# Head gates of the block-key mixer: three products of rounded halves in place of one full-precision product

## The reference

```python
xn = rmsnorm(x, mix_norm[i])
proj = xn @ w_in                      # 256 x 1024 times 1024 x 2608
q, kc, vc, ks, vs, kw, vw, gates = jnp.split(proj, cuts, axis=-1)
gates = jax.nn.sigmoid(gates.reshape(bsz, s, g, r, 3) + b_gate.reshape(g, r, 3))
```

## Time and profile before

| | us |
|---|---|
| median of 3 runs (lowest, highest) | 2112.36 (2108.29, 2113.53) |
| the profiled execution, its own time | 2112.04 |
| its span, first to last instruction | 2110.2 |
| PE busy in the span | 2084.3 (99%) |
| DVE busy | 1541.8 (73%) |
| ACT busy | 1289.6 (61%) |
| POOL busy | 61.5 (3%) |

### The profile page before, as it was taken

The page is one execution under the profiler, slowest core; times in us unless marked ns, Lnnn a source line. Parts: engine busy times, 40 slices in busy tenths (PEclk is TensorE's granted clock), DMA queues, the critical chain, the costliest instruction groups (busy, mean ns, idle before and its releaser), DMA issues.

```text
span 2110.2 us, 33620 instructions
## 1 busy us (share of the span) xinstructions
PE 2084.3 (99%) x12545; PEld 1790.8 (85%) x12545; DVE 1541.8 (73%) x2787; ACT 1289.6 (61%) x2170; POOL 61.5 (3%) x51
## 2 busy tenths in 40 slices
PE   8999999999999999999999999999999999999999
PEld 7888988888888877888888897888887888988887
DVE  6777888677766677766877677587677776868676
ACT  6656766556555367655665677565565555666555
POOL 0001000000000400000000001000000000000000
PEclk9999999999999999999999999999999999999999
DMA  7553445454555532555455351145445544445452
GB/s 271 185 209 127 159 180 189 180 192 167 210 181 166 180 121 111 193 196 190 166 194 197 126 193 61 71 174 206 180 155 196 203 181 155 164 155 187 180 195 94
DMA packets 74827, 360.76 MB, mean 171 GB/s; under 512 B 17000, under 2 KB 18024, under 8 KB 43816
## 3 DMA queue, kind: packets, MB, share of 16 engines
q1 hardware_dynamic: 74240, 358.08, 46.8%
q0 software_dynamic: 128, 0.26, 0.0%
q10 hardware_dynamic: 296, 0.27, 0.0%
HBM read 357.54 MB, written 1.05 MB: 170 GB/s over the span
## 4 chain that ended last, share of the span: by engine, by line
PE 89%; DVE 5%; ACT 4%; issue 1%; DMA 1%; SPq 0%; DVEq 0%; POOL 0%; ACTq 0%; POOLq 0%
PE ps L203 87%; ACT work L193 2%; DVE WL L121 2%; PE ps L208 2%; DVE work L121 1%; ACT WH L193 1%; DMA ring<-wts 1%; ACT XBt L193 1%; DVE XBt L132 1%; DVE work L132 0%; DVE small L121 0%; DVE small L132 0%; DVE Xt L132 0%; DVE work L158 0%; DVE Xt L121 0%
## 5 line engine op out<-in xcount | busy, mean ns | idle before, releaser
L203 PE MATMUL ps<-XBt,WH 128*128 128x512 f32 (+1 forms) x4144 | 1197.3, 355 | 4.4 <-DVE XBt L132 1.9
L121 DVE TENSOR_TENSOR WL<-ring,WH 128x1024 fp32r<-128x1024 f32 (+2 forms) x653 | 791.3, 1212 | 345.3 <-ACT WH L193 297.9
L193 ACT ACTIVATE WH<-ring 128x1024 fp32r<-128x1024 f32 (+1 forms) x667 | 698.8, 1048 | 345.4 <-PE ps L203 260.9
L203 PE MATMUL ps<-XBt,WL 128*128 128x256 f32 x3352 | 886.5, 280 | 0.0
L203 PEld LDWEIGHTS ps<-XBt,WH 128*128 128x128 f32 x4144 | 718.5, 190 | 105.9 <-DVE WL L121 4.5
L203 PEld LDWEIGHTS ps<-XBt,WL 128*128 128x128 f32 x3352 | 635.6, 190 | 26.6
L203 PE MATMUL ps<-WH,HHt 128*128 128x512 f32 x712 | 278.8, 392 | 0.9 <-DVE WL L121 0.7
L203 PE MATMUL ps<-WH,HLt 128*128 128x512 f32 x712 | 277.2, 389 | 0.0
L203 PE MATMUL ps<-WL,HHt 128*128 128x512 f32 x712 | 277.1, 389 | 0.0
L193 ACT ACTIVATE work<-ps 128x256 f32<-128x256 f32 (+4 forms) x444 | 179.3, 408 | 60.4 <-PE ps L203 21.8
L193 ACT ACTIVATE work<-work 128x256 f32<-128x256 f32 (+6 forms) x222 | 98.7, 445 | 171.1 <-DVE work L121 167.9
(11 more groups left out here) (137 smaller groups left out, 1076.8 us busy)
## 6 DMA issues: line engine op xcount, KB each, us to landing
ring<-wts SPq DMA_DIRECT2D x240, 1024.0 KB, 5.8
ring<-wts SPq DMA_DIRECT2D x185, 512.0 KB, 3.8
ring<-wts SPq DMA_DIRECT2D x10, 256.0 KB, 5.0
ring<-wts SPq DMA_DIRECT2D x1, 1152.0 KB, 5.0
Xt<-x SPq DMA_DIRECT2D x4, 256.0 KB, 5.7
out<-Xt SPq DMA_DIRECT2D x4, 256.0 KB, 2.0
ring<-wts SPq DMA_DIRECT2D x1, 768.0 KB, 6.5
work<-wts SPq DMA_DIRECT2D x1, 512.0 KB, 4.6
```

The source lines that it names most:

```text
L121: self.done(self.e and self.e.tensor_tensor(out, a, b, op), inc)
L193: self.done(self.e and self.e.activation(out, a, f, **kw), inc)
L203: inst = self.e and self.e.matmul(out, l, r, start=start, stop=stop)
```

## The change

POOL no longer makes XF. The gates' weights NG are cut into halves as the other weights are: ACT writes the high half into HHt, DVE the low half into HLt. PE makes the gates from XH, XL and these halves with `mm3`, in the same place of its order, into the same PSUM regions.

```diff
-            norm = unscaled(t, vec("mix_norm", 8, 16), prev, True, whole=True)
+            norm = unscaled(t, vec("mix_norm", 8, 16), prev, True)
...
+            def gates_pe(P):
+                nh, nl = v3(HHt[:, 0:384], 8), v3(HLt[:, 0:384], 8)
+                for i in range(2):
+                    ps.take(f"nsa_gt{i}")
+                    P.wait_ge("nsa_gt:lo", *ps.free(f"nsa_gt{i}"))
+                    for kt in range(8):
+                        P.mm3(ps[f"nsa_gt{i}"][:, 0:48], XH[:, kt, hs(i)], XL[:, kt, hs(i)], nh[:, kt, :], nl[:, kt, :], kt == 0, kt == 7,
+                              inc=f"nsa_gt{i}" if kt == 7 else None)
+                    ps.give(f"nsa_gt{i}", f"nsa_gt{i}.e")
...
-                tm_pe(P, "nsa_gt", v3(NG, 8), 8, 48, XF, "nsa_gt:ld", "nsa.xf")
+                gates_pe(P)
...
             def act(A):
                 norm.act(A)
-                for piece in ("nsa_c0", "nsa_c1", "nsa_q0.0", "nsa_q0.1"):
+                hi(A, ahead("nsa_c0"))
+                A.wait_ge("nsa_gt:ld", f"f1.1.{NFF - 1}:d")
+                A.act(HHt[:, 0:384], NG, ACT.Copy, inc="nsa_gt:hi")
+                for piece in ("nsa_c1", "nsa_q0.0", "nsa_q0.1"):
                     hi(A, ahead(piece))
...
                 gather_dve(V, 1)
+                V.wait_ge("nsa_gt:hi")
+                V.tt(HLt[:, 0:384], NG, HHt[:, 0:384].bitcast(F32), SUB, inc="nsa_gt:lo")
                 V.set(KC, 0.0)
...
             def pool(G):
-                norm.pool(G)
                 G.wait_ge(f"{t}.dg")
```

## The result

| | before | changed |
|---|---|---|
| median, first comparison | 2111.11 (18 runs) | 2114.78 (18 runs) |
| ratio of the two, 95% interval | | 1.0015, 1.0008 to 1.0021 |
| profiled execution | 2112.04 | 2114.09 |

The change makes the kernel slower by 0.15%, some 3.2 us by the ratio (1.7 to 4.4) and 3.7 by the medians. 2115.0 had been forecast. It lies well inside the 0.3% that was called no change.

The account below looks back on a forecast made before the run. PE, busy 99% of the span, was taken to bound the kernel. Relief and cuts -0.15, gate passes +2.0 and clock +0.85 made +2.7 us, forecast 2115.0 (own range 2113 to 2117, whole range 2109.0 to 2119.0).

Parts of the forecast that it names:

- The relief left over: At PE's start of q1.0: of DVE's lead of 0.55 us, only 0.15 is left after the new cut.
- the gather's wait: On DVE before q0.1: the gather waits for POOL's cut, leaving a lead of about 0.55 us of 1.15.
- Parts 1 and 2: DVE ahead of q0.1: without XF, DG comes 1.15 us earlier; after the gather's wait, 0.55 is left.
- Part 3: DVE's new cut HLt before the cut of q1.0: about 0.56 us, 0.6 with the gap, using up the lead.
- Part 4: ACT's new cut HHt fits a gap of 1.86 us and costs nothing; at most 0.6 without that cover.
- Part 5: PE's gates: 48 passes at 0.117 us instead of 32 at 0.112, +2.0 us (bounds -2.5 and +5.5).
- Rival B: At PE's gates: rounded narrow passes cost their columns, not their weights, gates take 1.1 to 2.7 us; time 2108.8; chance 6%.
- Part 6: Granted clock near the gates: a likelier, longer fall to 1.2 GHz, +0.85 us (bounds -1.7 and +3.5).
- Rival C: Clock stays low through the gates and after, for 10 us: +5.3 in all, 2117.6; chance 14%.
- Rival A: DVE's relief wins: no gather collision, mostly no clock fall behind the gates; -0.3, 2112.1; chance 17%.

Follow-up runs that it names:

- e5: The changed kernel with DVE's cut HLt moved behind the cut of q1.0; 2115.32 us, ratio 1.0018 to the kernel before.
- e1: The changed kernel with POOL's four additions of XF put back, read by nobody; 2114.82 us, ratio 1.0018 to the kernel before.
- e4: The changed kernel with gate operands exchanged: 48 weight columns stand, 256 tokens move, 24 passes and two transposes; 2111.01 us, ratio 0.9996 to the kernel before.
- e6: e4 with DVE's cut HLt moved behind the cut of q1.0; 2110.28 us, ratio 0.9996 to the kernel before.
- e8: e4 with HLt's cut behind that of q1.0 and k0.0 cut before the gates are finished; 2113.58 us, ratio 1.0008 to the kernel before.

## Why the prediction was right

The sign, the size and the place were right, and so was each mechanism: relief, used-up lead, dearer gates, longer low clock. That +2.7 came so near to the measured 3.2 to 3.7 is in part luck. The relief left over and the clock were taken too small, the gather's wait and the passes too large, and the clock's share, 2.2 against +0.85, lies outside the 0 to 1.7 of the forecast's own range, though inside the bound of +3.5.

*Parts 1 and 2, relief.* Both stalls went as forecast, 1.15 us together. Of this 0.98 reached the steps that make DG: the operation behind the two-column addition starts 0.22 us after it now (0.04 before), and why is not shown. PE is 0.62 ahead behind the DG wait, where 0.61 was taken. The gather now starts at 703.68, inside POOL's cut that ends at 704.16. The chain lists its halves:

```profile
703.68 1.26 DVE work L121
704.97 1.01 DVE work L121
```

So it waited 0.25 us where 0.6 was taken (its first half took 1.01 before). It did wait as the cut does: behind POOL's end the gather's half takes 0.78 of its 1.01 us, and the cut of q0.0 takes 1.09 of its 1.23. What was mis-sized is the overlap, 0.48 us. PE starts q0.1 at 18.66 on the ruler where it was 19.41: 0.75 ahead (0.98 less 0.25), between the ends of 0.55 and 1.15. The collision of the cuts of q0.0 stays, 3.19 us.

*Part 3, HLt.* 0.56 us, as said, and it is late next: PE waits 0.35 for the cut of q1.0. Left of the lead is 0.34, not 0.15. e5 and e1 fix both sides: 26.49 without the cut in the way, 27.63 without the lead.

*Part 4, HHt.* 0.52 us, in ACT's gap; PE waits for nothing behind it.

*Part 5, passes.* 0.111 to 0.113 each, +1.7 against the +2.0 taken. The weights set it, and not a least cost of any pass: the eight passes with 64 weight columns and 60 columns moved start at 744.33 and the next pass stands at 744.71, so they cost under 0.05 each. The turned passes, 48 weight columns and 256 tokens, cost 0.116 and number half. Rival B is out.

*Part 6, clock.* The term that was mis-sized: +0.85 was taken. Over all executions that list it the mean clock is 0.99785 before (99 runs) and 0.99669 changed (29 runs), that is 4.9 us more of low time. By the ruler 3.41 us low cost 1.51, not the half of 1.7, so this is an estimate of 2.2 us. With 1.7 - 0.34 it makes +3.6; the means of these runs differ by 3.1. At an equal mean clock of 0.997 the changed kernel is 1.2 us slower (2113.89 against 2112.65), at 0.998 it is 0.96; the clock is listed to 0.001, which is worth some 2 us, so these two are rough. By both ways more than half of the loss is the clock. The traces show only a part of the 4.9: 2.6 more near the gates (6.0 in the four with 48 passes in one run, 3.4 in the three of the kernel before), and nothing more around 1300 us (5.1 against 5.7). By the traces alone the clock is 1.2 us of some 2.6. Where the rest lies is open, and seven traces are few.

Rival C, low for 10 us, came only when the passes were doubled. Rival A's times occur as single executions (the lowest is 2111.64) but not as the median.

## What to carry to other kernels

Removing work from an idle engine can gain time where a busy engine's two-operand additions wait for it; count the gain at the engine on the path, behind the next cut in line (here 1.15 us became 0.75 and then 0.34). A matmul that loads 128 weight columns to move 48 costs its weights. Exchanging the operands saved 2.1 us of passes here and the fall at the gates with them; laying such passes between wide ones saved the fall alone. When a change of 0.1% is judged, compare fixed marks in several traces and the runs at equal mean clock, since most of the scatter of whole times goes with the clock.

## What was unexpected

- Most of the scatter of the kernel before goes with the granted clock: its 99 runs average 2109.5 us at a mean clock of 0.999, 2111.0 at 0.998, 2112.7 at 0.997 and 2115.5 at 0.996. Their standard deviation is 1.8 us over all and 0.8 about these four means.
- Low clock costs less than half: 1.51, 3.2 and 6.5 us for 3.41, 6.83 and 13.65 us low. A rounded 256-column pass goes from 0.12 to 0.213, not to twice 0.12 (from 732.18 on, in q1.1 of the changed kernel).
- Two thin runs of the same length (3.6 us) in one kernel fell one at a time, each in some traces.
- The clock did not fall at the gates when their passes used 48 of the array's columns and moved 256 (e4, e6 and e8, one trace each).
